# Reordering the matmuls of a k tile so that two output halves take turns

## The reference

```python
z = x @ W['w_in'][l]                                   # 2048 -> 13828 columns
proj = jnp.einsum('blkc,kcd->blkd', branches, W['w_branch'][l])   # four mixers, 512 -> 2048 each
merged = jnp.einsum('blkd,blkd->bld', gates, proj)
x = layer_norm(DEEPNORM_ALPHA * x + merged @ W['w_out'][l], ...)  # 2048 -> 2048
gate_ff, up_ff = jnp.split(x @ W['w_ffn_up'][l], 2, axis=-1)      # 2048 -> 2 x 5632
x = layer_norm(DEEPNORM_ALPHA * x + (jax.nn.silu(gate_ff) * up_ff) @ W['w_ffn_down'][l], ...)
```

## Time and profile before

| | us |
|---|---|
| three runs, median (lowest, highest) | 1710.65 (1709.58, 1711.78) |
| the profiled execution | 1711.33 |
| its span, first to last instruction | 1709.5 |
| PE busy, share of the span | 99% |
| DVE, ACT, POOL busy, share of the span | 63%, 47%, 8% |

### The profile page before, as it was taken

One profiled execution on the slowest core, in us unless ns is written; L12 is line 12 of the kernel. 1 busy time (PEld: TensorE's weight loads), 2 busy tenths in 40 slices (PEclk: granted clock), 3 DMA queues, 4 the chain that ended last, 5 costly groups with the idle time before them and its releaser, 6 DMA issues.

```text
span 1709.5 us, 33400 instructions
## 1 busy us (share of the span) xinstructions
PE 1698.2 (99%) x13814; PEld 1650.2 (97%) x13814; DVE 1074.9 (63%) x1271; ACT 798.5 (47%) x894; POOL 138.7 (8%) x148
## 2 busy tenths in 40 slices
PE   9999999999999999999999999999999999999998
PEld 8999998999999999999999999999999999999997
DVE  7898897666558666555687874444444444454655
ACT  5654544656444444444355563444443343333433
POOL 7200000000012555000000000000000000000000
PEclk9999999999999999999999999999999999999998
DMA  8565577776758887666556555555555555555552
GB/s 264 153 207 164 161 218 239 234 229 206 216 154 244 277 267 246 184 183 184 174 180 196 180 172 185 182 176 182 182 176 181 182 176 182 185 175 170 190 178 78
DMA packets 309558, 329.75 MB, mean 193 GB/s; under 512 B 12223, under 2 KB 289987, under 8 KB 309188
## 3 DMA queue, kind: packets, MB, share of 16 engines
q1 hardware_dynamic: 308044, 326.59, 62.0%
q10 hardware_dynamic: 1400, 1.54, 0.3%
HBM read 322.31 MB, written 5.77 MB: 192 GB/s over the span
## 4 chain that ended last, share of the span: by engine, by line
PE 97%; DVE 2%; DMA 1%; issue 0%; ACT 0%; SPq 0%; DVEq 0%
PE ps L790 15%; PE ps L1152 15%; PE ps L791 15%; PE ps L1153 15%; PE ps L792 15%; PE ps L1151 15%; PE ps L863 1%; PE ps L1040 1%; DVE w_split L1664 1%; DMA w_in_ring<-in_w_in 1%; PE ps L898 1%; PE ps L828 0%; PE ps L813 0%; PE ps L806 0%; PE ps L1231 0%; PE ps L841 0%
## 5 line engine op out<-in xcount | busy, mean ns | idle before, releaser
L2353 DVE TENSOR_TENSOR w_lo<-w_raw,w_hi 128x1024 fp32r<-128x1024 f32 x264 | 322.8, 1225 | 326.4 <-ACT w_hi L1548 323.4
L1664 DVE TENSOR_TENSOR w_split<-w_in_ring,w_split 128x1024 fp32r<-128x1024 f32 x276 | 352.7, 1281 | 236.2 <-ACT w_split L1252 225.7
L790 PE MATMUL ps<-xh,w_split 128*128 128x264 f32 x1680 | 481.3, 287 | 2.9 <-DVE w_split L1664 2.9
L1548 ACT ACTIVATE w_hi<-w_raw 128x1024 fp32r<-128x1024 f32 x264 | 279.3, 1060 | 438.0 <-PE ps L1153 433.3
L791 PE MATMUL ps<-xl,w_split 128*128 128x264 f32 x1680 | 477.9, 284 | 0.0
L792 PE MATMUL ps<-xh,w_split 128*128 128x264 f32 x1680 | 476.5, 284 | 0.0
L1252 ACT ACTIVATE w_split<-w_in_ring 128x1024 fp32r<-128x1024 f32 x276 | 291.3, 1060 | 353.8 <-DMA w_in_ring<-in_w_in 266.1
L790 PEld LDWEIGHTS ps<-xh,w_split 128*128 128x128 f32 x1680 | 315.9, 188 | 19.2 <-issue 12.0
L1152 PE MATMUL ps<-x1l,w_hi 128*128 128x264 f32 x1152 | 327.6, 284 | 0.0
L1153 PE MATMUL ps<-x1h,w_lo 128*128 128x264 f32 x1152 | 326.8, 284 | 0.0
L1151 PE MATMUL ps<-x1h,w_hi 128*128 128x264 f32 x1152 | 325.8, 283 | 0.0
(11 more groups left out here) (502 smaller groups left out, 2148.9 us busy)
## 6 DMA issues: line engine op xcount, KB each, us to landing
w_in_ring<-in_w_in SPq DMA_DIRECT2D x210, 512.0 KB, 3.8
w_raw<-in_w_ffn_up SPq DMA_DIRECT2D x176, 512.0 KB, 3.5
w_raw<-in_w_ffn_down SPq DMA_DIRECT2D x88, 512.0 KB, 3.4
kv<-in_cache_k SPq DMA_DIRECT2D x64, 258.0 KB, 3.7
w_in_ring<-in_w_branch SPq DMA_DIRECT2D x32, 512.0 KB, 4.4
kv<-in_cache_v SPq DMA_DIRECT2D x64, 256.0 KB, 3.7
w_in_ring<-in_w_out SPq DMA_DIRECT2D x32, 512.0 KB, 3.4
x_t<-in_x SPq DMA_DIRECT2D x8, 264.0 KB, 6.9
```

The lines of the kernel that those rows point to most:

```text
L790: nc.tensor.matmul(out, w_split[:, slot, 0, c], right_h[:, k, :], start=first, stop=False)
L1548: A_(w_hi[:, n % RING2, :], raw[:, n % RING2, :], ACT.Copy).then_inc(sem("hi2"), 1)
L1664: V.tensor_tensor(w_split[:, slot, 1, :], w_in_ring[:, slot, 1, :], w_split[:, slot, 0, :], ALU.subtract).then_inc(sem("lo_done"), 1)
L2353: V.tensor_tensor(w_lo[:, n % RING2, :], raw[:, n % RING2, :], w_hi[:, n % RING2, :], ALU.subtract).then_inc(sem("lo2"), 1)
```

## The change

Within a k tile the six matmuls are issued in another order. Before, one half does its three products, then the other half. After, each of the three products is done for half 0 and half 1 in turn. Two lists, `cols` (the weight columns of each half) and `out` (its bank), are made when the program is built; they cost no instruction. The start flag (first k tile of a pass) and the stop flag (last one) stay with the same products. `last_products` is untouched.

```diff
                 first, last = k == 0, k == count * per - 1
+                cols = [slice((kk * tiles + half) * P, (kk * tiles + half) * P + P) for half in range(tiles)]
+                out = [PS[:, BANK(p) + half, 0:TOK] for half in range(tiles)]
                 for half in range(tiles):
-                    out = PS[:, BANK(p) + half, 0:TOK]
-                    c = slice((kk * tiles + half) * P, (kk * tiles + half) * P + P)
-                    nc.tensor.matmul(out, w_split[:, slot, 0, c], right_h[:, k, :], start=first, stop=False)
-                    nc.tensor.matmul(out, w_split[:, slot, 0, c], right_l[:, k, :], start=False, stop=False)
-                    ins = nc.tensor.matmul(out, w_split[:, slot, 1, c], right_h[:, k, :], start=False, stop=last)
+                    nc.tensor.matmul(out[half], w_split[:, slot, 0, cols[half]], right_h[:, k, :], start=first, stop=False)
+                for half in range(tiles):
+                    nc.tensor.matmul(out[half], w_split[:, slot, 0, cols[half]], right_l[:, k, :], start=False, stop=False)
+                for half in range(tiles):
+                    ins = nc.tensor.matmul(out[half], w_split[:, slot, 1, cols[half]], right_h[:, k, :], start=False,
+                                           stop=last)
             ins.then_inc(sem("used"), 1)
```

## The result

| | before | after |
|---|---|---|
| median of 20 runs (lowest, highest), us | 1710.95 (1708.5, 1717.2) | 1716.06 (1713.24, 1720.93) |
| the profiled execution, us | 1711.33 | 1718.87 |
| its span, us | 1709.5 | 1716.9 |

The ratio is 1.0029, with a 95% interval of 1.0022 to 1.0036: slower by 5.1 us, more than the 0.2% that can be told from no change. The time lies inside the stated range, but the likeliest case, within 0.2%, did not come; the outcome "slower" had been given 0.23.

The account below looks back on a forecast made before the run. PE's matmul steps were taken to bound the kernel; 1,052 k tiles x 2.0 ns + 1,096 x 0.0 = +2.1 us on 1710.65 gave about 1712.5 us. Range 1707 to 1714, for 8 in 10 1704 to 1718.

Parts of the forecast that it names:

- the likeliest case, within 0.2%: Whole kernel: time within 0.2% (3.4 us) of no change, chance 0.61.
- The bound, the counts, the waits: PE busy 1698.2 of 1709.5 us, waits 4.0 us; matmul and weight load counts stay, other effects worth nothing.
- four kinds of neighbours: Steps in a k tile, by same or other weights, bank, row; loop means 120.5, 121.9, 122.1, 121.35 ns.
- (a): Twice per k tile, high-by-high to high-by-low: same weights, same bank, other row; mean 120.5 ns in the loop.
- The term for the second part: Program's second part, gate and up loop and rest: 1,052 k tiles, each 2.0 ns longer.
- the term for the first part: Program's first part: 1,096 k tiles, 729.9 ns before and after, 0.0 difference.
- Both places that I read for it: Two `ff` chunks in one bank, 121.4 ns steps; final layer norm's L1217 and L1228, both 1.05 us: banks cost nothing.
- the rival with steps near 124 ns: Big matmuls: a bank change costs, 2.6 ns more per step, +33 us, 1744; chance 0.04.
- the one with a stall in a bank, at 111: Big matmuls: accumulating twice running into a bank stalls; steps could fall to 111 ns, -135 us, 1576; chance 0.02.
- The pair with the same weights was cheap: K tile's same-weights steps: losing them costs +3.9 us, 1714.6, at worst +9.5 us, 1720; chance 0.18.
- The sequence of rows and weights sets the small stalls: Big matmuls: last chunk's 1.0 ns gain taken over, -13 us, 1698, half of it 1704; chance 0.14.
- The clock: Rival: PE pauses halve the granted clock; a tenth of the run so adds 83 us; chance 0.01.

Follow-up runs that it names:

- f_bank: Against the kernel before, only the banks of a k tile's six matmuls changed, to 0 1 0 1 0 1: loop 396.21 us, ratio 1.0000.
- f_weights: Against the kernel before, only the weights put in the order of after, halves in turn: loop 396.21 us, ratio 1.0001.
- g_halves: Against the kernel before, every chunk takes half 0 through its four k tiles, then half 1: median 1707.45 us, ratio 0.9976.

## Why the prediction was right or wrong

- **The bound, the counts, the waits: right.** PE's steps are the time, no wait or load was added, and the loop's stretch carries the same matmuls without a gap.
- **"Whether a step's length depends on what stands before and after it": the step that failed.** I sorted the steps before into four kinds of neighbours (same or other weights, bank, row) and priced the new order by the means of two of them: 3 x 122.1 + 3 x 121.35 = 730.3 ns per k tile. The new order's own means in the loop are 122.4, 122.3 and 120.7 for half 0 to half 1, and 120.6, 122.3 and 123.3 for the way back: 731.7. A kind of neighbours has no price of its own. The sign of it stood in the prediction: (a) took 119.6 ns in half 0 and 121.5 in half 1, and I took this for something that averages out over a k tile. f_bank and f_weights show that two of the three marks by which I sorted do nothing, and the four kernels with other orders that the third, same row or other row, does nothing by itself either. What decides is where in memory the rows of the sequence start, which is none of the three marks. By the prediction's own sign (steps of both kinds within 1 ns of 121.7) it was not met: the means run from 120.6 to 123.3.
- **The sum: right in sign, too small.** +2.1 us against +5.1 measured. The term for the second part, +2.0 ns per k tile, was +3.3 in the loop; the term for the first part, 0.0, was 2.3 (six steps at 0.39 ns more). The forecast within 0.2% rested on the first part's 0.0. That 1716.06 lies in the range all the same is luck: the range reaches to 1718 for the sake of the rival with the same weights, whose cause was not at work.
- **Banks: right.** Both places that I read for it said that a bank change neither costs nor saves, and f_bank confirms it to 0.01 us in the loop. They were weaker evidence than they looked, since the rows that they read differ from the loop's as well. So the rival with steps near 124 ns fell, and so did the one with a stall in a bank, at 111.
- **"The pair with the same weights was cheap": the time it gave (1714.6, at worst 1720) was met by 1716.06, its cause was not.** f_weights takes the pair away and the loop stays at 396.21 us. That half 1's steps of that kind were not short, which I held against it, was the better reading.
- **"The sequence of rows and weights sets the small stalls": the cause, with two mistakes.** The weights have no part in it, and I gave it only to the faster side, because the only other order in the trace, the last chunk of the earlier trace rows, was faster. A mechanism that hangs on the sequence has no side until the sequence itself is read. The price from that chunk, 1.0 ns off each step, was too large as well: the same order in every chunk takes 396.21 us in the loop, as before, and gains 4.1 us in all, where 13 were given. One chunk was too small a sample: the chunk just ahead of it, in the usual order, already took 2.79 us (its first and last matmul below) against the 2.80 of the chunk that I compared it with, and with the same order in all other chunks the last one itself takes 2.79 in place of 2.77.

```profile
1683.62 0.28 PE L1151 MATMUL ps<-hh,w_hi 128*128 128x264 f32 x1
...
1686.41 0.28 PE L1153 MATMUL ps<-hh,w_lo 128*128 128x264 f32 x1
```

- **The clock: right.** 1.00 throughout the loop in every kernel. Its fall near the end was misread as one "where PE waits": between 1695 and 1700 us PE is busy for 5.00 of 5.00 us, in the matmuls of the layer norm, and the mean granted clock of that stretch (the view's 0.83, columns as in the earlier trace rows) has fallen already.

```profile
1695.00:1700.00 5.00, 5.00 (x16) 3.02 (x16) 4.34 (x7) 3.50 (x7) 0.00 (x0) 0.83 0.28 108
```

What stays open is why a step depends on the rows' starts, which sequence of starts is cheap, and how far back it counts. The traces give the sum over a sequence and not the rule. Tensors laid at other addresses, which would show how far below 121 ns a step can be brought, were not tried; nor was the loop without the splits of ACT and DVE beside it, so whether these take part is not shown.

## What to carry to other kernels

Where PE is busy without a gap, compare two orders by the length of a long stretch of the same matmuls; here it came out the same to a hundredth of a us, where whole runs of one kernel differ by 0.5%. Before an order of matmuls is changed, note for each matmul where its moving row starts in memory, and keep that sequence, or vary it on purpose; banks and weights could here be put in any order at no cost. Half by half through a chunk (all k tiles of one bank, then of the other) was the best of the six orders run here; that holds for these addresses, and another kernel has to be measured.

## What the runs showed of the hardware

- A matmul of 264 fp32r columns steps at 121.1 to 122.5 ns on average at the full clock, by the sequence of the rows' start addresses (395.31 to 399.80 us for 3,264). Half by half, a low row 0 bytes from its high row and one 17 x 256 or 83 x 256 bytes from it give the same 395.31 us; 66.5 x 256 gives 396.21. The out pass, with 66 x 256, has the steps of the former in all three orders.
- The lengths return when all starts move by 33 x 256 bytes (710.8 ns for the third and the eleventh k tile before), and not at 16.5 x 256 (734.2 for the seventh).
- The same 24 matmuls can take 2.77 or 2.79 us by the sequence that ran ahead of them (the last chunk, before and g_halves).
- The mean step of the loop did not depend on whether the bank or the weights change from one matmul to the next (396.21 us in before, f_bank and f_weights), nor on whether a row is read once or three times in succession (395.31 us in both).
